# Split products for the input projection, and the end of a pass re-ordered, in a two-block transformer kernel

## The reference, cut to what matters

```python
h = rms_norm(x, norm_mix_g[l])
proj = h @ w_in[l]                      # (256, 1024) @ (1024, 5120)
c_a, c_g, q_r, f_r, i_r, g_r, gate_c, gate_r = jnp.split(proj, SPLITS, axis=-1)
y_conv = conformer_conv_branch(c_a, c_g, conv_w[l], conv_b[l], ...)
y_rec = hgrn2_branch(q_r, f_r, i_r, g_r, lower_bounds[l], ...)
```

## Time and profile before

| | |
|---|---|
| median of 3 runs | 2205.52 us (2202.16 to 2206.67) |
| the profiled execution, its own time | 2204.83 us |
| its span in the profile | 2202.9 us |
| granted clock of TensorE, mean | 0.976 of full |
| PE busy, share of the span | 2058.0 us, 93% |
| DVE, ACT busy | 1203.4 us, 820.7 us |
| read from memory | 537.56 MB, 244 GB/s over the span |

### The profile page before, as it was taken

How to read it: one execution, slowest core, us unless ns; L and a number is a source line. 1 busy time by engine, 2 the same in 40 slices (tenths; PEclk the granted TensorE clock), 3 DMA queues, 4 the chain that set the end, 5 groups by cost and what they waited for, 6 DMA issues and landing times. The chain is left out here.

```text
span 2202.9 us, 31510 instructions
## 1 busy us (share of the span) xinstructions
PE 2058.0 (93%) x12690; PEld 1612.5 (73%) x12690; DVE 1203.4 (55%) x1966; ACT 820.7 (37%) x1371; POOL 62.9 (3%) x72
## 2 busy tenths in 40 slices
PE   7999899889999888898889999999999999999998
PEld 6687659664444566676878888768888888888887
DVE  1185134454211234334567773477777777877776
ACT  2102224320111222222554453275555544545454
POOL 1000000000000000000000011001001000101000
PEclk9999999989999999899999999999999999999999
DMA  9997776259999999999545455115357554364441
GB/s 360 401 375 280 295 279 237 98 208 372 421 421 418 415 402 412 417 405 393 176 166 184 153 191 152 37 39 188 111 198 234 168 192 170 117 230 153 140 166 39
DMA packets 211160, 540.66 MB, mean 245 GB/s; under 512 B 8894, under 2 KB 105752, under 8 KB 186440
## 3 DMA queue, kind: packets, MB, share of 16 engines
q1 hardware_dynamic: 208264, 531.69, 64.3%
q0 software_dynamic: 2192, 6.57, 1.0%
q10 hardware_dynamic: 560, 0.38, 0.1%
HBM read 537.56 MB, written 1.05 MB: 244 GB/s over the span
## 5 line engine op out<-in xcount | busy, mean ns | idle before, releaser
L1217 PE MATMUL lo<-xs,wp 128*128 128x512 f32 (+1 forms) x3392 | 590.3, 336 | 11.3 <-DVE wp L2484 8.1
L1217 PEld LDWEIGHTS lo<-xs,wp 128*128 128x128 f32 x3392 | 514.3, 189 | 86.7 <-issue 12.5
L908 ACT ACTIVATE wp<-ring 128x1024 fp32r<-128x1024 f32 (+2 forms) x432 | 347.4, 828 | 251.3 <-PE hi L1217 142.2
L2484 DVE TENSOR_TENSOR wp<-ring,wp 128x1024 fp32r<-128x1024 f32 (+2 forms) x432 | 397.0, 939 | 12.0 <-ACT wp L908 11.9
L1217 PE MATMUL hi<-hs,wp 128*128 128x256 f32 (+1 forms) x1808 | 315.0, 335 | 6.2 <-DVE hs L2829 3.2
L1217 PEld LDWEIGHTS hi<-hs,wp 128*128 128x128 f32 x1808 | 272.9, 189 | 44.5 <-DVE hs L2829 3.5
L1217 PE MATMUL lo<-ring,scratch 128*64 128x512 f32 (+1 forms) x1536 | 254.8, 596 | 15.3 <-DMA ring<-in_moe_w_up_dram 6.8
L1217 PEld LDWEIGHTS lo<-ring,scratch 128*64 128x64 f32 (+1 forms) x1536 | 79.8, 124 | 176.0 <-issue 162.1
L1217 PE MATMUL lo<-ht,ring 128*128 128x256 f32 (+1 forms) x640 | 136.4, 373 | 3.5 <-DMA ring<-in_w_in_dram 1.6
L1217 PEld LDWEIGHTS lo<-ht,ring 128*128 128x128 f32 x640 | 118.1, 192 | 23.0 <-ACT ht L1133 2.4
L2491 DVE TENSOR_TENSOR ring_r<-ring,home 128x1024 fp32r<-128x1024 f32 x52 | 63.0, 1223 | 131.0 <-ACT home L916 131.0
(11 more groups left out here) (437 smaller groups left out, 2377.1 us busy)
## 6 DMA issues: line engine op xcount, KB each, us to landing
ring<-in_mod_w_dram SPq DMA_DIRECT2D x72, 1024.0 KB, 13.6
ring<-in_moe_w_gate_dram SPq DMA_DIRECT2D x64, 1024.0 KB, 12.4
ring<-in_moe_w_up_dram SPq DMA_DIRECT2D x64, 1024.0 KB, 15.7
ring<-in_moe_w_down_dram SPq DMA_DIRECT2D x64, 1024.0 KB, 15.1
ring<-in_ffn_w_gate_dram SPq DMA_DIRECT2D x55, 1024.0 KB, 6.3
ring<-in_ffn_w_up_dram SPq DMA_DIRECT2D x55, 1024.0 KB, 9.0
ring<-in_ffn_w_down_dram SPq DMA_DIRECT2D x50, 1024.0 KB, 10.2
ring<-in_w_in_dram SPq DMA_DIRECT2D x20, 1024.0 KB, 12.9
```

The costliest lines, as they stand in the source:

```text
L908: act.activation(wp[:, q % SLOTS, 0, k:k + w.shape[1], :], w, ACT.Copy).then_inc(piece_hi, 2 // len(parts))
L1217: return pe.matmul(dst, lhsT, rhs, start=start, stop=stop, **kw)
L2484: tt(wp[:, q % SLOTS, 1, k:k + w.shape[1], :], w, wp[:, q % SLOTS, 0, k:k + w.shape[1], :].bitcast(F32), ALU.subtract).then_inc(piece_lo, ...
```

## The change

The products of the input projection become split products. Each of the ten blocks is cut into four pieces (`IN_PIECES` = 40). ACT rounds a piece into one of three homes (`gate_r` and the two halves of `side_r`), DVE writes the rest over the piece in the ring, PE multiplies three times, and the rounding of piece q waits until piece q - 3 is done (`in_done`). The normed input is split too, into `x_split`. DVE's convolution taps, its scan and ACT's Sigmoid and Silu are placed by hand between the roundings and rests; the transfer of `masks` goes to another place in the buffers and waits for the first norm, that of `cx` waits for the last piece. At a pass's end ACT squares the last piece before it rounds, fetches the root's table at d = 2 and not at d = 6, `keep_busy` there runs once and not twice, and for uses 1 to 5 the last piece goes by `late_step` into one half of its bank, so that DVE adds it in one instruction.

```diff
@@ -175,7 +175,7 @@
 zero = sb("zero", [P, 1])
-masks = ht[:, :, T:T + P]
+masks = side[:, 1, TT * CW:TT * D].rearrange("p (k n) -> p k n", k=KC)
@@ -364,6 +364,17 @@
+IN_PIECES = 40
+def in_weights(q):
+    n, i = u_in(q // 4), q % 4
+    by_rows = q // 4 == 4
+    w, rest = (v.rearrange("p (k n) -> p k n", k=KC) for v in (unit_of(n), ring_r[:, n % RING, :]))
+    w, rest = (v[:, 2 * i:2 * i + 2, :] if by_rows else v[:, :, i * P:i * P + P] for v in (w, rest))
+    home = (gate_r[:], side_r[:, 0, 0:D], side_r[:, 0, D:2 * D])[q % 3]
+    return w, home.rearrange("p (k n) -> p k n", k=2 if by_rows else KC), rest
@@ -637,14 +649,16 @@
     pool.wait_ge(rows_loaded, 16 * 17)
-    for dst, src in ((masks, k_masks), (desc[:, 0:PER_GROUP + 4 * BATCH], k_desc), (moe_gain, norm_ffn_g[0].rearrange("(p c) -> p c", p=P)), (scratch[:, 13440:13440 + P + PLACES], k_rank)):
+    for dst, src in ((desc[:, 0:PER_GROUP + 4 * BATCH], k_desc), (moe_gain, norm_ffn_g[0].rearrange("(p c) -> p c", p=P)), (scratch[:, 13440:13440 + P + PLACES], k_rank)):
         pool.dma_start(dst, src).then_inc(consts_loaded, 16)
-    pool.dma_start(cx, mem[0].rearrange("(t p) d -> p t d", p=P)).then_inc(mem_loaded, 16)
...
     pool.dma_start(router_b[:, GROUPS:], router_expert_b[0].partition_broadcast(P)).then_inc(consts_loaded, 16)
-    pool.wait_ge(mix_scan, 1)
+    pool.wait_ge(norm_turned, 4)
+    pool.dma_start(masks, k_masks).then_inc(consts_loaded, 16)
+    pool.wait_ge(in_done, IN_PIECES)
+    pool.dma_start(cx, mem[0].rearrange("(t p) d -> p t d", p=P)).then_inc(mem_loaded, 16)
@@ -720,16 +734,29 @@
+    def in_round(q):
+        if q % 4 == 0:
+            wait_unit(act, u_in(q // 4))
+        if q >= 3:
+            act.wait_ge(in_done, q - 2)
+        w, home, _ = in_weights(q)
+        act.activation(home, w, ACT.Copy).then_inc(in_hi, 1)
...
     norm_stats(0, x, 0)
+    in_round(0)
     act.wait_ge(cols_ready, 5)
+    for c in range(KC):
+        act.wait_ge(norm_turned, c // 2 + 1)
+        act.activation(x_split[:, 0, c], hi[:, c // 2, (c % 2) * T:(c % 2 + 1) * T], ACT.Identity, scale=col(R_MIX + c)).then_inc(norm_ready, 1)
+    in_round(1)
+    in_round(2)
...
-    norm_out(0, 0, col(R_MIX, KC))
@@ -743,18 +770,22 @@
     for j in range(10):
+        for q in range(4 * j + 3, min(4 * j + 6, IN_PIECES)):
+            in_round(q)
...
                                    3: (lo[:, 2:4, :], cum, ACT.Sigmoid, mix_f), 5: (lo[:, 2:4, :], grT, ACT.Silu, mix_g)}[j]
-            wait_used(act, u_in(j))
+            act.wait_ge(in_done, 4 * j + 4)
...
         elif j >= 6:
-            wait_used(act, u_in(j))
+            act.wait_ge(in_done, 4 * j + 4)
...
             act.activation(dst, lo[:, 2 * (j % 2):2 * (j % 2) + 2, :], ACT.Sigmoid).then_inc(mix_gate, 1)
+        if 4 * j + 6 < IN_PIECES:
+            in_round(4 * j + 6)
@@ -1011,8 +1042,18 @@
         act.activation(sq[:, d % 2], src[:, d], ACT.Square).then_inc(sq_done, 1)
-        if d == KC - 2:
+        if d == 2:
...
+    def rounded_and_squared(q, use, d, e, meanwhile=None):
+        if d < KC - 1:
+            round_next(q + d)
+        if meanwhile:
+            meanwhile(d)
+        squares(use, d, e)
+        if d == KC - 1:
+            round_next(q + d)
@@ -1023,11 +1064,12 @@
         for d in range(KC):
+            if use is not None:
+                rounded_and_squared(down_q(f, p, 0), use, d, E_FFN[f] + KC * p, meanwhile)
+                continue
...
                 meanwhile(d)
-            if use is not None:
-                squares(use, d, E_FFN[f] + KC * p)
@@ -1190,8 +1231,7 @@
     for d in range(KC):
-        round_next(Q_CMO + d)
-        squares(5, d, E_CMO)
+        rounded_and_squared(Q_CMO, 5, d, E_CMO)
@@ -1221,12 +1261,33 @@
-    def to_features(n, dst, rhs, chunks, last=True):
-        for f in range(4):
-            for k in range(chunks):
-                ins = mm(dst(f), as_cols(n)[:, k, f * P:f * P + P], rhs(k), k == 0, k == chunks - 1)
-        ins.then_inc(unit_used[n % RING], 1)
+    def in_features(q, dst):
+        _, home, rest = in_weights(q)
+        for k in range(KC):
+            if q == 0:
+                pe.wait_ge(in_xlo, k + 1)
+            xh, xl = (x_split[:, a, k, :] for a in range(2))
+            ins = mm(dst, rest[:, k, :], xh, k == 0, False, skip_group_check=True)
+            if q % 4 == 3 and k == KC - 1:
+                ins.then_inc(unit_used[u_in(q // 4) % RING], 1)
+            mm(dst, home[:, k, :], xh, False, False, skip_group_check=True)
+            ins = mm(dst, home[:, k, :], xl, False, k == KC - 1, skip_group_check=True)
+        ins.then_inc(in_done, 1)
+    def in_rows(q):
+        _, home, rest = in_weights(q)
+        for t in range(TT):
+            for k in range(2):
+                c = q % 4 * 2 + k
+                xh, xl = (x_split[:, a, c, t * P:t * P + P] for a in range(2))
+                ins = mm(lo[:, t, :], xh, rest[:, k, :], c == 0, False, skip_group_check=True)
+                if q % 4 == 3 and t + k == TT:
+                    ins.then_inc(unit_used[u_in(q // 4) % RING], 1)
+                mm(lo[:, t, :], xh, home[:, k, :], False, False, skip_group_check=True)
+                ins = mm(lo[:, t, :], xl, home[:, k, :], False, c == KC - 1, skip_group_check=True)
+        ins.then_inc(in_done, 1)
@@ -1296,16 +1353,17 @@
-    pe.wait_ge(col_math, 2)
     for j in range(10):
-        n = u_in(j)
-        wait_unit(pe, n)
...
             pe.wait_ge(*before[j])
-        if j == 4:
-            to_rows(n, lambda t: lo[:, t, :], ht_tile)
-        else:
-            to_features(n, pair(lo, 2 * (j % 2)), ht_all, KC)
+        for q in range(4 * j, 4 * j + 4):
+            pe.wait_ge(in_lo, q + 1)
+            if j == 4:
+                in_rows(q)
+            else:
+                in_features(q, pair(lo, 2 * (j % 2))(q % 4))
+        if j == 0:
+            pe.wait_ge(col_math, 2)
@@ -1731,11 +1789,22 @@
-    def piece(q, dst, n, rhs):
+    def late_step(q, dst, k, n, rhs):
+        w = wp[:, q % SLOTS]
+        ins = mm(dst, w[:, 0, k, :], rhs[:, k, 0], k == 0, False, skip_group_check=True)
+        if k < len(freed(q)):
+            ins.then_inc(unit_used[freed(q)[k] % RING], 1)
+        mm(dst, w[:, 0, k, :], rhs[:, k, 1], False, False, skip_group_check=True)
+        ins = mm(dst, w[:, 1, k, :], rhs[:, k, 0], False, k == n - 1, skip_group_check=True)
+        if k == n - 1:
+            ins.then_inc(piece_done, 1)
+    def piece(q, dst, n, rhs, of=step):
...
         for k in range(n):
-            step(q, dst, k, n, rhs)
+            of(q, dst, k, n, rhs)
@@ -1768,14 +1837,17 @@
         if d == KC - 1:
-            keep_busy(lo[:, 0], 2)
+            keep_busy(lo[:, 0], 1)
...
             pe.wait_ge(ev_done, e + d - 3)
-        piece(q + d, hi[:, d % 4, :], n, hs)
+        if use is not None and d == KC - 1:
+            piece(q + d, hi[:, d % 4, 0:T], n, hs, late_step)
+        else:
+            piece(q + d, hi[:, d % 4, :], n, hs)
@@ -2114,36 +2173,74 @@
     link(ts(subln[:], col(R_SUBLN), 1.0 - LAM_INIT, None, ALU.mult))
-    norm(0, 0, x, 0, col(R_MIX, KC))
+    def in_rest(q):
+        dve.wait_ge(in_hi, q + 1)
+        w, home, rest = in_weights(q)
+        tt(rest, w, home.bitcast(F32), ALU.subtract).then_inc(in_lo, 1)
+    taps_done = [0]
+    def conv_tap():
+        j = taps_done[0]
+        taps_done[0] += 1
+        for c in range(CC if j < TAPS else 0):
+            if j == 0:
+                ins = ts(acc[:, c, :], upad[:, c, 0:T], col(R2_TAPS + c, 1, 1), col(R_CONVB + c), ALU.mult, ALU.add)
+            else:
+                dve.wait_ge(conv_step, j * CC + c + 1 - CC)
+                ins = stt(acc[:, c, :], upad[:, c, j:j + T], col(R2_TAPS + j * CC + c, 1, 1), acc[:, c, :], ALU.mult, ALU.add)
+            ins.then_inc(conv_step, 1)
+    norm_rows(0, x)
+    in_rest(0)
+    for c in range(KC):
+        dve.wait_ge(norm_ready, c // 2 * 2 + 2)
+        ps = hi[:, c // 2, (c % 2) * T:(c % 2 + 1) * T]
+        stt(x_split[:, 1, c], ps, col(R_MIX + c), x_split[:, 0, c].bitcast(F32), ALU.mult, ALU.subtract).then_inc(in_xlo, 1)
+    in_rest(1)
+    in_rest(2)
...
-    dve.wait_ge(mix_cg, 1)
-    wait_used(dve, u_in(0))
-    tt(upad[:, :, TAPS - 1:TAPS - 1 + T], lo[:, 0:2, :].rearrange("p a (b t) -> p (a b) t", b=2), cg_sig, ALU.mult).then_inc(mix_u, 1)
...
-    dve.wait_ge(mix_u, 1)
-    for c in range(CC):
-        ts(acc[:, c, :], upad[:, c, 0:T], col(R2_TAPS + c, 1, 1), col(R_CONVB + c), ALU.mult, ALU.add).then_inc(conv_step, 1)
-    with dve.Fori(1, TAPS) as j:
-        for c in range(CC):
-            dve.wait_ge(conv_step, j * CC + (c + 1 - CC))
-            stt(acc[:, c, :], upad[:, c, bass.ds(j, T)], cols[:, 1, bass.ds(j * CC + c, 1)], acc[:, c, :], ALU.mult, ALU.add
-                ).then_inc(conv_step, 1)
+    for j in range(10):
+        for q in range(4 * j + 3, min(4 * j + 6, IN_PIECES)):
+            in_rest(q)
+            if j >= 2:
+                conv_tap()
+        if j == 1:
```

(63 more changed lines are left out.)

14 lines of the change are left out of this document (removed).

## The result

The changed kernel took 2184.4 us as the median of four runs (2179.9 to 2189.2) against 2205.7 for the kernel before: a ratio of 0.9907, 95% interval 0.9883 to 0.9931. Run again it gave 2188.4 (six runs) against 2206.0 (17 runs), 0.9924, interval 0.9906 to 0.9942. The two gains are 21.3 and 17.6 us, and the forecast of 19.9 lies between them. The profiled execution was the fastest of its four: 2179.9 us, span 2178.1.

What follows compares the result with a forecast made beforehand. PE, always busy from 60 us, was taken to bound the projection; -17.2 us there and -2.7 at the pass ends, -19.9 together, gave 2185.5 us; likeliest 2181 to 2190, with rivals 2176 to 2195.

Steps and rivals of the forecast that it cites:

- A block at 11.65 us: Input projection: a block becomes 96 float32r products of 121.3 ns, 11.65 us on PE, where it took 14.08.
- Memory and PE in the rounds: Projection rounds: memory needs 15.7 us for three units, PE 15.3; PE, later overall, decides, and the projection ends at 169.0.
- Pieces hidden from PE: Projection: rounding (1.05 us) and rest (1.22) of a piece are hidden in a steady state; DVE's sum is 106 in about 150.
- pieces wait for rests: Projection: a sign that would show the prediction wrong, PE's pieces waiting for DVE's rests; no size given.
- The clock: Projection, before block 2: 2.7 us of PE idling lowers the clock for a while, costing 1.5 us (bounds 0 and 2.7).
- The chain over `mix_u`: Before block 2: unit at 50.8 us, two roundings, a rest beside the Sigmoid, then the `mix_u` product, ending at 55.4.
- the clock is granted below 1.00: Projection: a sign that would show the prediction wrong, PE's granted clock below 1.00 there.
- It reaches the end: Stages after the projection: they move with PE, the experts start 17 us earlier; no loss taken, bound 5 us.
- the cover of 3 to 4 us: Level stage after the projection: its units, 8 us late in all, stay covered by 3 to 4 us.
- The ends: Pass ends: use 0 -1.2 us, use 1 +0.3, uses 2 to 5 0.45 sooner each (-1.8); together -2.7.
- The table's drain: End of use 1: the Trainium skill's 1.38 us drain after a table switch, left out; with it 1.4 us worse.
- Rivals: Whole kernel: memory or clock takes more (0.17, 2194 us); more gained (0.15); gain given back (0.04); split not paying (0.04).

Runs made afterwards that it cites:

- `after_again`: The changed kernel run once more without any edit; ratio 0.9924 against the kernel before.
- `front_only`: The changed kernel with its split input projection, but the ends of the passes as before; 2190.6 us, ratio 0.9934 against the kernel before.
- `ends_only`: The kernel before with only the four edits at the ends of the passes, projection in float32 as before; 2205.5 us, ratio 1.0000.
- `half_mod_before`: The kernel before with half the bytes in the units of the first seven `mod_w_2` products; projection ended at 182.95 us and not 186.08.
- `late_mod_evac`: The changed kernel with seven mod products and their units later, and block 1's Sigmoid and `mix_u` product ahead of block 2's preparation; 2181.2 us, ratio 0.9891.

## Why the prediction was right, step by step

- **A block at 11.65 us**: 11.7 where nothing waited (block 2, 54.30 to 66.04; the last three 133.90 to 168.71, 34.8 where 35.0 was forecast). The rate of 121 ns from the earlier trace rows held. The 109 ns of the Trainium skill (TensorE: Matmul & The Clock Gate, "Wait — 56ns, not 53.3ns?") are not seen here: three products of a k-slice take 0.36 us, 120 ns each.
- **Memory and PE in the rounds**: right up to block 4, and again from block 5. The rate was 401 and 399 GB/s where 400 was taken. By memory's own pace block 7 could start at 131.6 in the sum (50.8 + 2.3 + 5 x 15.7); its unit came at 129.27, and with the same 2.3 us that is 131.6. That PE would be later and decide was right too: block 7 started at 133.90 (forecast 134.0). The rounds took 15.28, 15.70, 17.54 (with the small turn of 0.9 and a wait of 1.61), 15.76 and 15.32 us.
- **Pieces hidden from PE**: wrong in one place. The prediction compared DVE's whole sum with the time it has, 106 us in 150, and called "pieces wait for rests" a sign of being wrong. One piece of block 4 did wait, for 1.61 us, since DVE's work for block 3 stood ahead of its rest (0.97 in `after_again`, 0.39 in `front_only`). As PE sets the pace from block 5 on, that wait reaches the end of the projection; with that work behind the rest, DVE would have had the piece near 90.2 (88.94 + 1.22) and PE no wait. This is an estimate; no run has that order.
- **The clock**: the loss of 1.5 us was put behind the wait on `mix_u`. The chain over `mix_u` was right, 4.68 us from the unit to block 2 for 4.6. But the wait at its end was only 1.01 us, as the unit came at 49.6 and not at 50.8 and PE was ready at 53.3 and not at 52.7, and it cost nothing. The loss came in the first gap instead: 3.64 us of idling before block 1, then a clock of 0.70 over 5.6 us, which is 1.7 us (0.30 x 5.6; block 1 took 13.3, 1.6 above 11.7). So the sign "the clock is granted below 1.00" came as well. At the end of the projection it cost nothing: PE was ready for block 2 a microsecond before the chain over `mix_u` was, even so. The prediction placed block 1 at 37.4 behind a product that ends near 32 and gave that gap no clock at all. Taken together the two slips cancel: block 2 started 1.1 us sooner and at full clock, and the waits in the rounds took these 2.6 us back. That 168.55 lies so near 169.0 is in this part luck. One reading behind the 1.5 does not hold: the prediction put block 0's 15.57 us down to the clock, but it was granted at 1.00 from 17 to 38 us; in `ends_only` and `half_mod_before` the same block took 14.08 behind the same idle time of 1.23. Why it ran longer once stays open.
- **It reaches the end**: yes. From the end of the projection to the experts' first transfer it is 310.8 us before and 310.9 after, and 306.1 to 310.9 in all kernels whatever their front, with `ends_only` (306.1) at the low end. Against a scatter of 4.7 us one execution says little; the medians of `front_only` say that 10 to 19 us arrive. The level stage kept 391 GB/s and a DMA share of 1.00. That the cover of 3 to 4 us was as thin as worked out wasn't tested; at `late_mod_evac`, where the projection ends 9 us sooner still, the distance was 307.7.
- **The ends**: use 0 exact (-1.24 to -1.26 for -1.2). Uses 2 and 5 gave 0.63 and 0.68 by the second table. The forecast of 0.45 has 0.07 for the last piece's products in it, which this distance leaves out; 0.52 is to be compared. Uses 3 and 4 were treated as use 2, though PE waits for POOL in them as in use 1; like with like they gave 0.38. Use 1 was forecast 0.3 worse. Its end is 0.14 better, but its whole distance is 0.1 to 0.3 longer in short passes and 0.3 to 0.4 in long ones: the sign was right. The delay by the early table is there, 0.5 us at that end (`best`); it was taken as 0.9. So the sum of 2.7 came out near 3, with single terms off by up to 0.2.
- **The table's drain**: the tiny activation stands right behind the load (here in use 2), and use 1 came out at most 0.4 worse, so the 1.38 us that the Trainium skill (ScalarE: Activation LUTs, "What ACT_TABLE_LOAD costs") adds are not seen on this path.

```profile
1477.21 1.28 ACT L1046 ACT_TABLE_LOAD   x1
1478.51 0.20 ACT L1046 ACTIVATE small<-eps 128x1 f32<-128x1 f32 x1
```

- **Rivals**: memory took no more than forecast, the clock 1.7 and not 2.7; the medians show nothing given back. Apart from the 1.61 us in block 4 the split's preparation holds PE nowhere for more than 0.2 us once block 2 has started, also not in the last blocks, where DVE has taps in front of its rests.
- The profiled execution gained 24.9 us: 17.5 up to the experts, 0.2 from there to the root of use 0, 4.2 between the roots and 2.9 behind the last. Some 6 of the last two are use 4's distance and the last stretch at their lower values (192.50 for 195.88, and 200.6 for 203.5). `front_only` has both without the edits at the ends (192.83 and 200.2), `after_again` has neither (195.53 and 203.7). That part belongs to the execution, not to the change.

## What to carry to other kernels

When an engine's work in a stage shrinks, ask what the ring's units cost per round at the measured rate: here 24.8 us taken from PE were worth 17.5. Re-ordering the units so that no other transfers stand between the first two blocks, and the Sigmoid ahead of two roundings, ended the stage 8.8 us sooner still, of which 3 to 7 us show in the medians. Check an engine that prepares pieces piece by piece, from the arrival of each unit, and not by its sum over the stage: DVE was busy for 28 of the 40 us from 60 to 100 and still late once. Look at each idle gap of PE that the new order opens, and not only at the one just analysed, for what the clock may take behind it. At the end of a pass look use by use for who comes last; the same four edits were worth 1.2, 0.1, 0.6, 0.4, 0.4 and 0.7 us at the ends of six uses. Compare passes only with passes of the same form.
